# Reversed score rows of the odd tiles: put in order by a store to memory and a row gather, in place of two products with a reversal matrix

## The chip, the cores and the metric

The kernel runs on one core of a Trainium2 chip. The metric is the device time of one execution in microseconds (us), lower being better. Two chained blocks of a transformer-like model are computed for 512 tokens of width 1024, all in float32; large products are made as three products of rounded halves (high by high, low by high, high by low).

## The reference, cut to what matters

The second block contains a gated linear attention. Only its scores matter here; the kernel works in chunks of 128 tokens, which gives the same result as the reference's 64.

```python
def gla_chunked(q, k, v, log_f):
    ...
    def step(state, inp):
        qb, kb, vb, gb = inp
        cum = jnp.cumsum(gb, axis=-2)
        diff = cum[..., :, None, :] - cum[..., None, :, :]
        decay = jnp.exp(jnp.where(causal, diff, -jnp.inf))
        scores = jnp.einsum('bhtd,bhsd,bhtsd->bhts', qb, kb, decay)
        o_intra = jnp.einsum('bhts,bhsv->bhtv', scores, vb)
        o_inter = jnp.einsum('bhtd,bhdv->bhtv', qb * jnp.exp(cum), state)
        ...
        return new_state, o_intra + o_inter
```

## The kernel before

The 512 tokens are four tiles of 128. The first 51 weight blocks (n = 0 to 50) are taken in an order written out by hand. For each block every engine has its own straight list: SyncE loads the raw weights, ScalarE rounds them to the high half (`split`, helper line L1252), VectorE subtracts to get the low half (`lower`, L1808), TensorE multiplies (`fm_block`, through `three`, lines L594 to L596) and ScalarE and VectorE drain the banks. Beside each block an engine's `side(n)` does a piece of the attention work. In TensorE's list `side(n)` comes before the block's products, except for the blocks in `MID`, where it comes between the block's two tiles.

The gated attention's scores SC (16 tiles of 128x128, index head * 4 + token tile, rows are source tokens) are made level by level: n = 26 to 37 multiply (`gla_pairs`, L942) and VectorE merges the product under a mask (`level_merge`, L2188). For the odd token tiles the keys were reversed (KREV, KEP), so that the rows of the odd score tiles stand in reverse order. The level merges end in block 37. Then:

- n = 38 (GO - 2), TensorE: `scores_turn`, two products of the 128x128 reversal matrix by four odd score tiles each (L951) into banks 6 and 7.
- n = 39 (GO - 1), TensorE: `kdec_turn` (16 transposes of the decayed keys, L749). ScalarE: two copies of banks 6 and 7 back to SC (L1467), `chunk_split(0)` and `chunk_split(1)` (high halves of the values, L1385, and of the scores, L1386), then four copies of the transposed keys (L1475). VectorE: the low halves of the same (L1808), in `chunk_split` and `k_dec_lower`.
- n = 40 (GO) and after, TensorE: `gla_out(j)` for j = 0 to 3, which for j = 0 waits until the four transposed banks are drained by `k_dec_lower`. ScalarE squares the output (L1394), GpSimd computes the reciprocal root (`rstd`, L2850 and L2851), VectorE scales by it. ScalarE and VectorE split chunk j + 2 beside `gla_out(j)`.

GpSimd's list is short: the small roots, the loads with accumulation, a few broadcasts. Between the last root of the layer norm in block 33 and the first of `gla_norm` in block 40 it has nothing. `x1_spilled` is the semaphore of an earlier store of the residual to memory (16 when done, L2905). `tables_in` counts three small table loads at the start, the last of them the reversal matrix (L3000).

Of the kernel before, what the change touches and what calls it, by code (L numbers as in the profile page):

```python
# [15 lines left out]
P = 128  # L16
S = 512
# [84 lines left out]
def two_blocks(nc, a, out, x1_spill, m_spill):  # L102
# [47 lines left out]
    REVERSAL = place("reversal", [P, P])  # L150
# [64 lines left out]
    KEP = at("k_decayed_left_halves", [P, H * S // 2], XS + 16 * K1)  # L215
    KREV = at("k2_odd_tiles_reversed", [P, H * S // 2], XS + 12 * K1)
# [93 lines left out]
    with ctx:  # L310
# [258 lines left out]
        def two(t):  # L569
            return t.rearrange("p (t c) -> p t c", t=2)  # L570

# [6 lines left out]
        def _(pe):  # L578
# [366 lines left out]
            def scores_turn():  # L945

                for half in range(2):
                    drained(pe, ("lv", LEVELS - 1, half))
                for i in range(2):
                    dst = take(6 + i, ("scR", i))  # L950
                    give(pe.matmul(quarters(dst[:, :]), REVERSAL[:, :], SC[:, 2 * i + 1::TT, :], start=True, stop=True), ("scR", i))  # L951

# [111 lines left out]
            def side(n):  # L1064
# [14 lines left out]
                if n == GO - 2: scores_turn()  # L1079
# [153 lines left out]
        def _(act):  # L1233
# [149 lines left out]
            def chunk_split(j):  # L1383

                act.activation(V2H[:, j, :], V2[:, j, :], ACT.Copy).then_inc(chunk_hi, 1)  # L1385
                act.activation(SCH[:, :, j, :], SC[:, j::TT, :], ACT.Copy).then_inc(chunk_hi, 1)  # L1386
# [20 lines left out]
            def side(n):  # L1407
# [55 lines left out]
                if n == GO - 1:  # L1463
                    act.wait_ge(kd_done, 1)
                    for i in range(2):
                        b = full(act, ("scR", i))
                        ins = act.activation(SC[:, 2 * i + 1::TT, :], quarters(b[:, :]), ACT.Copy)  # L1467
                        free(ins, ("scR", i))
                    for i in range(2):
                        drained(act, ("scR", i))  # L1470
                    chunk_split(0)
                    chunk_split(1)
# [324 lines left out]
        def _(dve):  # L1797
# [409 lines left out]
            def chunk_split(j):  # L2207
# [4 lines left out]
                lower(SCL[:, :, j, :], SC[:, j::TT, :], SCH[:, :, j, :]).then_inc(chunk_lo, 1)  # L2212
# [624 lines left out]
        def _(pool):  # L2837
# [85 lines left out]
            for j in range(TT):  # L2923
                pool.wait_ge(ln_var, j + 1)
                rstd(RST[:, j:j + 1], MV[:, j, 1:2], 1, 1.0, LN_EPS)
            for j in range(TT):
# [29 lines left out]
        def _(sp):  # L2956
# [43 lines left out]
            sp.dma_start(REVERSAL[:, :], a["c_reversal"]).then_inc(tables_in, 16)  # L3000
# [81 lines left out]
def constants():  # L3082
# [3 lines left out]
    for l in range(LEVELS):  # L3086
# [6 lines left out]
            "c_masks": masks, "c_reversal": (s == P - 1 - t).astype(np.float32), "c_pool_edge": edge.astype(np.float32)}  # L3093
# [33 lines left out]
```

## Time and profile before

| what | value |
|---|---|
| median of 3 runs | 1060.89 us (1060.86 to 1061.44) |
| the profiled execution, its own time | 1060.83 us |
| its span, first to last instruction | 1059.0 us |
| TensorE matmul busy | 1049.3 us, 99% of the span |
| VectorE, ScalarE, GpSimd busy | 73%, 51%, 9% |
| mean granted TensorE clock | 0.999 of 2.4 GHz |

The span and the execution's own time differ by 1.83 us, which lies outside the instructions. A busy share says how full an engine's row is; the waits of an engine say whether it was ever late; and the chain that ended last says which engine's work, in order of time, adds up to the span.

### The profile page before, as it was taken

What the parts mean: (1) busy time and instruction counts of PE and PEld (TensorE: products, weight loads), DVE (VectorE), ACT (ScalarE), POOL (GpSimd) and SP (SyncE); (2) the same over time, 40 slices, a digit from 0 to 9 for tenths busy, and PEclk for the clock granted to TensorE, in tenths of its full rate; (3) what the DMA queues carried; (4) which work ended last, traced back from release to release, by engine and by line L of the source; (5) the groups of instructions that cost most, each with busy time, mean ns of one, the idle gap of its engine ahead of it and who ended that gap; (6) DMA issues with size and microseconds to landing.
All of it is one profiled execution on the core that took longest, in us unless ns stands there. A gap on an engine that the chain in (4) does not pass through costs nothing.

```text
span 1059.0 us, 13875 instructions
## 1 busy us (share of the span) xinstructions
PE 1049.3 (99%) x5688; PEld 906.5 (86%) x5688; DVE 777.9 (73%) x878; ACT 536.0 (51%) x620; POOL 91.5 (9%) x106
## 2 busy tenths in 40 slices
PE   9999999999999999999999999999999999999997
PEld 8788888888888888888888888888999999888885
DVE  5778856547976787777877455588887777897897
ACT  7575642453544644255434633352656656655560
POOL 1301000000012010001100000014000000220200
PEclk9999999999999999999999999999999999999999
DMA  9847412223863755323222222262132343999962
GB/s 325 242 114 166 145 52 74 90 80 105 212 141 108 219 121 160 119 80 100 82 78 80 80 80 80 102 218 79 50 111 80 103 137 121 179 206 251 180 218 80
DMA packets 95775, 138.89 MB, mean 131 GB/s; under 512 B 4988, under 2 KB 59772, under 8 KB 95584
## 3 DMA queue, kind: packets, MB, share of 16 engines
q1 hardware_dynamic: 77808, 97.49, 28.1%
q0 software_dynamic: 17616, 40.38, 18.8%
q8 instruction: 45, 0.74, 0.3%
q10 hardware_dynamic: 288, 0.13, 0.1%
q14 instruction: 18, 0.15, 0.0%
HBM read 133.79 MB, written 4.20 MB: 130 GB/s over the span
## 4 chain that ended last, share of the span: by engine, by line
PE 92%; DVE 4%; ACT 2%; DMA 1%; issue 1%; SPq 0%; DVEq 0%
PE bank L594 28%; PE bank L596 28%; PE bank L595 28%; PE bank L749 2%; DVE w_ff_lo L1808 1%; ACT w_ff_hi L1493 1%; PE bank L942 1%; PE bank L868 1%; PE bank L848 1%; PE bank L999 1%; PE bank L901 1%; PE bank L886 1%; DMA w_raw<-in_w_mem_kv 1%; PE bank L974 0%; DVE w_raw L2449 0%
## 5 line engine op out<-in xcount | busy, mean ns | idle before, releaser
L1808 DVE TENSOR_TENSOR w_lo<-w_raw,w_hi 128x2048 fp32r<-128x2048 f32 (+2 forms) x81 | 174.7, 2158 | 118.3 <-ACT w_hi L1252 97.8
L594 PE MATMUL bank<-act_t_hi,w_hi 128*128 128x512 f32 (+1 forms) x592 | 226.9, 383 | 0.0
L596 PE MATMUL bank<-act_t_hi,w_lo 128*128 128x512 f32 (+1 forms) x592 | 223.8, 378 | 0.0
L595 PE MATMUL bank<-act_t_lo,w_hi 128*128 128x512 f32 (+1 forms) x592 | 223.6, 378 | 0.0
L596 PEld LDWEIGHTS bank<-act_t_hi,w_lo 128*128 128x128 f32 x592 | 111.3, 188 | 20.9
L595 PEld LDWEIGHTS bank<-act_t_lo,w_hi 128*128 128x128 f32 x592 | 111.4, 188 | 20.4 <-issue 0.5
L594 PEld LDWEIGHTS bank<-act_t_hi,w_hi 128*128 128x128 f32 x592 | 111.4, 188 | 20.5 <-issue 0.5
L1252 ACT ACTIVATE w_hi<-w_raw 128x2048 fp32r<-128x2048 f32 (+1 forms) x48 | 88.9, 1854 | 31.8 <-PE bank L596 31.8
L594 PE MATMUL bank<-w_hi,hidden_hi 128*128 128x512 f32 x216 | 84.1, 389 | 0.0
L596 PE MATMUL bank<-w_hi,hidden_lo 128*128 128x512 f32 x216 | 84.0, 389 | 0.0
L595 PE MATMUL bank<-w_lo,hidden_hi 128*128 128x512 f32 x216 | 84.0, 389 | 0.0
L1808 DVE TENSOR_TENSOR w_ff_lo<-w_raw,w_ff_hi 128x1024 fp32r<-128x1024 f32 x49 | 59.9, 1223 | 28.3 <-ACT w_ff_hi L1493 28.3
L1493 ACT ACTIVATE w_ff_hi<-w_raw 128x1024 fp32r<-128x1024 f32 x49 | 51.7, 1056 | 43.6 <-DVE w_raw L2453 18.4
L1709 ACT ACTIVATE w_hi<-w_raw 128x2048 fp32r<-128x2048 f32 x28 | 53.5, 1911 | 30.3 <-DMA w_raw<-in_w_ff 26.5
L594 PE MATMUL bank<-act_t_hi,w_ff_hi 128*128 128x256 f32 x224 | 63.6, 284 | 0.4 <-DVE ff_hidden L2704 0.4
L596 PE MATMUL bank<-act_t_hi,w_ff_lo 128*128 128x256 f32 x224 | 63.4, 283 | 0.0
L595 PE MATMUL bank<-act_t_lo,w_ff_hi 128*128 128x256 f32 x224 | 63.4, 283 | 0.0
L596 PEld LDWEIGHTS bank<-w_hi,hidden_lo 128*128 128x128 f32 x216 | 40.5, 188 | 8.5
L595 PEld LDWEIGHTS bank<-w_lo,hidden_hi 128*128 128x128 f32 x216 | 40.5, 188 | 8.4
L594 PEld LDWEIGHTS bank<-w_hi,hidden_hi 128*128 128x128 f32 x216 | 40.5, 188 | 8.4 <-DVE w_lo L1808 0.2
L594 PE MATMUL bank<-h_sum_hi,w_ff_hi 128*128 128x256 f32 x168 | 47.5, 283 | 0.0
L595 PE MATMUL bank<-h_sum_lo,w_ff_hi 128*128 128x256 f32 x168 | 47.5, 283 | 0.0
(407 smaller groups left out, 2275.6 us busy)
## 6 DMA issues: line engine op xcount, KB each, us to landing
w_raw<-in_w_in SPq DMA_DIRECT2D x38, 1024.0 KB, 5.3
w_raw<-in_w_ff POOLq DMA_DIRECT2D x16, 1024.0 KB, 14.9
w_raw<-in_w_ff SPq DMA_DIRECT2D x28, 512.0 KB, 4.2
w_raw<-in_w_ff SPq DMA_DIRECT2D x13, 1024.0 KB, 8.3
w_vo_sums<-in_w_in POOLq DMA_DIRECT2D x8, 1024.0 KB, 9.2
w_raw<-in_w_out SPq DMA_DIRECT2D x8, 1024.0 KB, 5.1
w_vo_sums<-in_w_in SPq DMA_DIRECT2D x6, 1024.0 KB, 5.4
w_out_sums<-in_w_out POOLq DMA_DIRECT2D x4, 1024.0 KB, 8.9
```

Source lines behind the costliest of these rows:

```text
L594: pe.matmul(dst, lh, rh, start=start, stop=False, skip_group_check=onto)
L595: pe.matmul(dst, lh, rl, start=False, stop=False, skip_group_check=onto)
L596: return pe.matmul(dst, ll, rh, start=False, stop=stop, skip_group_check=onto)
L749: last = pe.transpose(dst[:, tile_of(i)], src(i), IDENT[:, :])
L848: last = pe.matmul(bank[b][:, c0:c0 + S - i * P], QK[:, 4 + h, tile_of(i)], QK[:, h, i * P:S], start=True, stop=True)
L868: last = pe.matmul(dst[:, c:c + P + 1], PP[h % 2][:, w:w + P], V[:, i, h, :], start=i == 0, stop=i == j)
L886: last = pe.matmul(dst[:, q:q + NMEM], QC[:, h, tile_of(j)], KM[:, h, :], start=True, stop=True)
L901: last = pe.matmul(dst[:, tile_of(h)], VM[:, m, tile_of(h)], PT[j % 2][:, 2 * h + m, :], start=m == 0, stop=m == MT - 1)
L1252: act.activation(WH[slot_of(n)][:, c0:w], raw_of(n)[:, c0:w], ACT.Copy).then_inc(w_hi, 1)
L1493: act.activation(UPH[g % FF1_SLOTS][:, :, :], up_place(i), ACT.Copy).then_inc(up_hi, 1)
L1709: act.activation(MH[split_slot(p)][:, :], MRAW[s][:, :], ACT.Copy).then_inc(w_hi, 1)
L1808: return dve.tensor_tensor(dst, src, hi.bitcast(f32), ALU.subtract)
```

## The change

The two products, ScalarE's two copies of them, and ScalarE's wait for its own copies are gone. GpSimd's queue, after the last root of the layer norm, waits until the last merge is done, stores the odd score tiles to memory (128 rows of 8 pieces of 512 B, 512 KB), waits until that store has landed and until the product ("sg", 7) is done (it read the table WST, whose place is used for the gather's target), and gathers the 128 rows of 4 KB back in reversed order into a new tile SCO. ScalarE waits for the gather ahead of `chunk_split(1)`, and the splits of chunks 1 and 3 read SCO. The table load of 64 KB becomes one of 128 row numbers.

```diff
-    REVERSAL = place("reversal", [P, P])
+    ROWS = place("reversed_rows", [P, 1], mybir.dt.uint32)
...
+    SCO = at("gla_scores_odd_tiles", [P, H, TT // 2, P], A + 72 * K1)
...
+        def scores_of(j):
+            return SCO[:, :, j // 2, :] if j % 2 else SC[:, j::TT, :]
...
-            def scores_turn():
-
-                for half in range(2):
-                    drained(pe, ("lv", LEVELS - 1, half))
-                for i in range(2):
-                    dst = take(6 + i, ("scR", i))
-                    give(pe.matmul(quarters(dst[:, :]), REVERSAL[:, :], SC[:, 2 * i + 1::TT, :], start=True, stop=True), ("scR", i))
...
-                if n == GO - 2: scores_turn()
...
-                act.activation(SCH[:, :, j, :], SC[:, j::TT, :], ACT.Copy).then_inc(chunk_hi, 1)
+                act.activation(SCH[:, :, j, :], scores_of(j), ACT.Copy).then_inc(chunk_hi, 1)
...
                     act.wait_ge(kd_done, 1)
-                    for i in range(2):
-                        b = full(act, ("scR", i))
-                        ins = act.activation(SC[:, 2 * i + 1::TT, :], quarters(b[:, :]), ACT.Copy)
-                        free(ins, ("scR", i))
-                    for i in range(2):
-                        drained(act, ("scR", i))
                     chunk_split(0)
+                    act.wait_ge(x1_spilled, 16 * 3)
                     chunk_split(1)
...
-                lower(SCL[:, :, j, :], SC[:, j::TT, :], SCH[:, :, j, :]).then_inc(chunk_lo, 1)
+                lower(SCL[:, :, j, :], scores_of(j), SCH[:, :, j, :]).then_inc(chunk_lo, 1)
...
+            for half in range(2):
+                drained(pool, ("lv", LEVELS - 1, half))
+            pool.dma_start(s_spill.rearrange("p (c t) -> p c t", t=P), SC[:, 1::2, :]).then_inc(x1_spilled, 16)
+            pool.wait_ge(tables_in, 16 * 3)
+            pool.wait_ge(x1_spilled, 16 * 2)
+            full(pool, ("sg", 7))
+            pool.indirect_dma_start(SCO[:, :, :, :].rearrange("p h c t -> p (h c t)"), None, s_spill[:, :],
+                                    bass.IndirectOffsetOnAxis(ROWS[:, :], 0)).then_inc(x1_spilled, 16)
...
-            sp.dma_start(REVERSAL[:, :], a["c_reversal"]).then_inc(tables_in, 16)
+            sp.dma_start(ROWS[:, :], a["c_rows"]).then_inc(tables_in, 16)
```

## Rows read from the trace of the kernel before

**Rows 1.** Busy time of each engine, share of the span, instructions.
```profile
PE 1049.3 (99%) x5688; PEld 906.5 (86%) x5688; DVE 777.9 (73%) x878; ACT 536.0 (51%) x620; POOL 91.5 (9%) x106
```
**Rows 2.** Waits of all engines: waiter, releaser, us in total, times, longest.
```profile
PE bank L594 <- DVE w_lo L1808: 1.0, 1, 1.0
PE bank L594 <- DVE ff_hidden L2704: 0.4, 2, 0.3
...
ACT w_hi L1709 <- DMA w_raw<-in_w_ff: 26.5, 12, 4.1
```
**Rows 3.** Chain that ended last, 564 to 580 us: start, us, what.
```profile
564.94 1.79 PE bank L999 x16
...
577.62 1.72 PE bank L951 x4
579.34 0.23 PE bank L594
```
**Rows 4.** The instructions of line L951: duration ns min/median/max, first and last start.
```profile
L951 PE MATMUL bank<-gla_scores,reversal x4: 591/592/592, 577.5 to 578.7; 128*128 128x512 f32 x4
```
**Rows 5.** TensorE in order of time, 577 to 580 and 602.75 us: start, us.
```profile
577.24 0.39 PE L596 MATMUL bank<-act_t_hi,w_lo 128*128 128x512 f32 x1
...
578.78 0.79 PE L594 MATMUL bank<-act_t_hi,w_hi 128*128 128x512 f32 x1
579.41 0.39 PE L595 MATMUL bank<-act_t_lo,w_hi 128*128 128x512 f32 x1
...
602.75 0.28 PE L594 MATMUL bank<-v_hi,gla_scores_hi 128*128 128x256 f32 x1
```
**Rows 6.** ScalarE in order of time, block 39: start, us.
```profile
592.69 1.07 ACT L1467 ACTIVATE gla_scores<-bank 128x512 f32<-128x512 f32 x2
593.86 1.06 ACT L1385 ACTIVATE v_hi<-v 128x1024 fp32r<-128x1024 f32 x1
...
595.34 1.04 ACT L1385 ACTIVATE v_hi<-v 128x1024 fp32r<-128x1024 f32 x1
```
**Rows 7.** GpSimd in order of time, 600 to 623 us; in brackets the idle time before.
```profile
606.99 0.84 POOL L2850 TENSOR_SCALAR rstd_tmp<-mean_squares 128x4 f32<-128x4 f32 x1 [84.49 <-ACT gla_o L1394]
...
621.68 0.20 POOL L2850 TENSOR_SCALAR rstd_tmp<-mean_squares 128x4 f32<-128x4 f32 x1 [12.76 <-ACT gla_o L1394]
```
**Rows 8.** VectorE in order of time, 568 to 608 us.
```profile
568.82 1.31 DVE L2188 COPY_PREDICATED gla_scores<-level_masks,bank 128x512 f32<-128x512 uint8 x1
...
575.01 2.29 DVE L2199 TENSOR_TENSOR decay<-cum 128x2048 f32<-128x2048 f32 x1
...
583.42 2.29 DVE L2205 TENSOR_TENSOR k_decayed<-k,decay 128x2048 f32<-128x2048 f32 x1 [0.94 <-ACT decay L1462]
...
596.78 1.22 DVE L1808 TENSOR_TENSOR v_lo<-v,v_hi 128x1024 fp32r<-128x1024 f32 x1
...
598.52 2.47 DVE L1808 TENSOR_TENSOR k_dec_t_lo<-bank,k_dec_t_hi 128x512 fp32r<-128x512 f32 x4
605.48 2.29 DVE L1808 TENSOR_TENSOR w_lo<-w_raw,w_hi 128x2048 fp32r<-128x2048 f32 x1 [4.49 <-ACT w_hi L1252]
```
**Rows 9.** GpSimd's issue of a transfer of 512 pieces of 512 B.
```profile
194.39 0.83 POOL L2887 DMA_DIRECT2D pool_w_sb<-in_pool_w  x1 [1.02 <-DVE mlstm_h L2054]
```
**Rows 10.** DMA issues of GpSimd's queue: count, KB each, median us to landing.
```profile
x_spill<-residual POOLq DMA_DIRECT2D x1, 2048.0 KB, 12.7
...
ln_b_all<-in_ln_b POOLq DMA_DIRECT2D x2, 512.0 KB, 14.2
...
w_s_by_source<-in_w_s_by_source POOLq DMA_DIRECT2D x1, 512.0 KB, 3.7
...
m_spill<-m_rows POOLq DMA_DIRECT2D x1, 8.0 KB, 4.1
```
**Rows 11.** Stretches: us, busy PE, PEld, DVE, ACT, POOL, clock, DMA share, GB/s.
```profile
568.00:573.00 5.00, 5.00 (x24) 4.15 (x23) 4.93 (x7) 3.88 (x4) 0.00 (x0) 1.00 0.61 179
573.00:578.00 5.00, 5.00 (x23) 3.98 (x22) 4.87 (x3) 0.34 (x1) 0.00 (x0) 1.00 0.09 31
```

More of the change, by code:

```diff
@@ L99, in block_list, with two_blocks @@
     return blocks
-def two_blocks(nc, a, out, x1_spill, m_spill):
+def two_blocks(nc, a, out, x1_spill, m_spill, s_spill):
+    import concourse.bass as bass
     from concourse import mybir
@@ L3092, in constants @@
     return {"c_ident": (s == t).astype(np.float32), "c_triu": (s <= t).astype(np.float32),
-            "c_masks": masks, "c_reversal": (s == P - 1 - t).astype(np.float32), "c_pool_edge": edge.astype(np.float32)}
+            "c_masks": masks, "c_rows": (P - 1 - s).astype(np.uint32), "c_pool_edge": edge.astype(np.float32)}
 def vector_columns(i):
@@ L3123 @@
     m_spill = nc.dram_tensor("m_spill", (H, S), mybir.dt.float32, kind="Internal").ap()
-    two_blocks(nc, a, out, x1_spill, m_spill)
+    s_spill = nc.dram_tensor("s_spill", (P, H * S // 2), mybir.dt.float32, kind="Internal").ap()
+    two_blocks(nc, a, out, x1_spill, m_spill, s_spill)
     r = run_bass_kernel_spmd(nc, [arrays], core_ids=[0])
```

## The prediction

> **What bounds the kernel now.** I read the busy times first: TensorE's matmul row is full, 1049.3 of 1059.0 us, and no other engine is above 73% [rows 1]. A full row need not be the bound, so I read the waits next. TensorE's waits are few: two groups with work of other engines, 1.0 us in the first blocks and 0.4 us in the feed-forward part [rows 2], none of them near the change. Third, the chain that ended last: around 577 us it consists of TensorE alone, and it holds the two products with the reversal matrix as one piece of 1.72 us, directly between ordinary products [rows 3]. So what TensorE no longer has to do in this stretch comes off the end, as long as nothing that it needs later becomes late.
>
> **What is removed from TensorE.** The two products are four records, two passes each [rows 4]. I price them by starts, not by durations, since the durations overlap. The ordinary product before them starts at 577.24, the next ordinary one is recorded at 578.78 but the one after that only at 579.41 [rows 5]. Ordinary starts are one chain piece of 0.23 us apart [rows 3], so without the products the step from 577.24 to 579.41 would take two pitches, 0.46 us, instead of 2.17: 1.71 us saved. The chain shows 1.72 [rows 3]. Bounds: not less than four ordinary pitches, 0.9 us, for four passes of the same 512 columns; not more than the four recorded durations, 4 x 0.592 = 2.37 us [rows 4]. I take 1.72, since two readings give it.
>
> **What is removed from ScalarE.** Two copies out of the banks take 1.07 us together, and with the hand-over 593.86 - 592.69 = 1.17 us pass before the values' split begins [rows 6]. ScalarE isn't on the path that sets the end here, so this is no gain in itself. I cost it at nothing, for TensorE's work hides it; it only gives ScalarE 1.17 us of room. Were that cover gone, it would be worth 1.17 us more.
>
> **What is added, and the room it has.** GpSimd has been idle for 84.49 us when its root at 606.99 begins, so nothing is queued behind its new waits until then [rows 7]. Its first wait ends with the last merge, 568.82 + 1.31 = 570.13 [rows 8]. The other wait, for the product ("sg", 7), ends with the group at 564.94 + 1.79 = 566.73 [rows 3], earlier, and costs nothing.
> Issue of the store: 1,024 pieces of 512 B. The nearest issue row, 512 such pieces, is 0.83 us [rows 9]; twice that is 1.7, my value.
> Store to landing: from below 4.1 us (the 8 KB store), from above 12.7 us (the 2 MB one) [rows 10]. It starts inside a weight load, since the DMA engines are 61% busy in 568 to 573 us and 9% in the next 5 [rows 11]. I take 6 us, near the small one: a quarter of the 2 MB transfer's bytes would be 3.2 us. Landed at 570.1 + 1.7 + 6 = 577.8.
> Gather, issue and landing: no row shows a gather. The nearest are loads of 512 KB into 128 rows, 3.7 us with free engines and 14.2 us at worst [rows 10]; a gather computes 128 addresses from a table, so I add 1 to 2 us and take 5.5 us. Landed at 583.3. With both transfers at their lower ends it is 570.1 + 1.7 + 4.1 + 3.7 = 579.6; with both at their upper ends, and an issue of 1.7 and one of 0.8 us, 570.1 + 12.7 + 14.2 + 2.5 = 599.5.
> When it is wanted: ScalarE's order begins 1.72 us earlier than before (it follows TensorE's drains) and without the copies. The first values' split then begins at 592.69 - 1.72 = 590.97; it and the scores' split took 595.34 - 593.86 = 1.48 us to the next start, so the new wait is reached at 592.45 [rows 6]. The gather has 22.3 us from the merge to there, and by my sum needs 13.2.
>
> **What waits behind it if it is late.** Call its landing G. On ScalarE behind the wait stand the second values' split (1.04 us), the scores' split, and the four copies of the transposed keys. VectorE's order behind that takes 598.52 + 2.47 - 596.78 = 4.21 us from its split of the second values to its last low half of the keys [rows 8]. It would end at about G + 1.1 + 4.2 = G + 5.3. TensorE's `gla_out(0)` waits for this and is due at 602.75 - 1.72 = 601.03 [rows 5]. So TensorE stalls only if G is after 595.7; it has lost the whole 1.72 us if G is 597.4, and the kernel is slower than before by 0.2% (2.1 us) if G is 599.5. The squares, roots and scaling of the output would then be late with TensorE, by the same amount and not more.
>
> **A rule against the change.** GpSimd's small operation at 606.99 took 0.84 us, and the same one at 621.68 took 0.20 [rows 7]. By the Trainium skill (SBUF — State Buffer, "SBUF: two separate sides") GpSimd and VectorE share a pair of ports, and GpSimd cannot write the descriptors of its transfers while VectorE holds it. The two durations agree with such a lock, for the first ended at 607.83, right after VectorE's weight split from 605.48 to 607.77 [rows 8].
> Whatever holds GpSimd, the rows say what it would do: VectorE is busy 4.93 and 4.87 us of the two stretches of 5 us from 568 to 578 [rows 11], its last long operation there ending at 577.30 [rows 8]. If the store can't be issued until then, it lands at 577.3 + 1.7 + 4.1 to 12.7, thus 583.1 at best. The gather's issue may then meet the operation at 583.42, which ends at 585.71 [rows 8], and land at 585.7 + 0.8 + 3.7 = 590.2. That is still 2.3 us before it is wanted, 5.5 before TensorE stalls. With 6 us for the store and 5.5 for the gather it is 585.0 and 591.2. Only this hold together with transfers near their upper ends is late.
>
> **Small things.** The table load shrinks from 64 KB to 512 B at the start, where no wait of TensorE hangs on it: nothing. The added traffic, 1 MB, falls beside weight loads that are wanted a block or more later; nothing. The later stretches hang on TensorE's progress, since each load is released by a split and each split by a product, so they should move by the same 1.72 us.
>
> **The sum.** The profiled execution took 1060.83 us with a span of 1059.0. Span after: 1059.0 - 1.72 = 1057.3; its own time 1059.1. The median of the runs is 0.06 above the profiled execution, so 1059.2 us, 0.16% less. Differences under about 0.2% (2.1 us) of this kernel cannot be told from no change; the forecast lies just inside that.
>
> **The rivals.**
> - *Forecast: the gather is hidden, TensorE saves its 1.72 us.* For it: the rows of the chain and of the starts, 9 us of room. 1058.8 to 1059.7. Chance 0.64.
> - *The products cost TensorE more than their pitch.* The record behind them is 0.79 us long instead of 0.39 [rows 5], and their durations add up to 2.37 [rows 4]; if that last value comes off, 1060.89 - 2.37 = 1058.5, and with a few tenths more from ScalarE's freed time in the feed-forward part, 1058.3. Against it: the starts behind them are already back at the ordinary pitch. Chance 0.20, faster by over 0.2%.
> - *The gain is swallowed later.* In the feed-forward part ScalarE waits for weight transfers 12 times, 26.5 us in all, and TensorE lost 0.4 us to VectorE there [rows 2]. Were that part paced by something that doesn't move with TensorE, 1060.9 would stay. Against it: what is loaded there is released by products and splits. Chance 0.05.
> - *The gather comes too late, the other side.* Its place is ScalarE's wait ahead of chunk 1, its point G = 597.4. Both transfers at their upper ends, free issue: G = 599.5, stall 3.8 us, time 1059.2 + 3.8 = 1063.0. With the issue held until 577.3 besides, G = 577.3 + 1.7 + 12.7 + 0.8 + 14.2 = 606.7, stall 11.0, time 1070.2. For it: no row shows a gather's price, and GpSimd can be held. Against it: the upper ends come from a transfer of four times the bytes and from moments with busy DMA engines, and here they are nearly free from 573 on [rows 11]. Chance 0.11, of which 0.02 lies between the thresholds and 0.09 beyond.
>
> **How the numbers follow.** Time 1059.2. Faster by over 0.2%: the second case, 0.20. Slower by over 0.2%: the last case's larger part, 0.09. Within: 0.64 + 0.05 + 0.02 = 0.71. The range for 8 times in 10 has the likeliest case and most of the second one; 1058.4 leaves out a little of the latter below, and 1060.4 leaves out the swallowed and the late cases above, 0.16 in all.
>
> **What the profile after would show.** The chain of TensorE around 577 us without the 1.72 us piece, and `gla_out(0)` at 601.0 instead of 602.75. GpSimd's store at 570.2, the gather's issue at 577 to 578 (past 583 if VectorE holds it), its landing by 584. ScalarE without a wait for DMA ahead of its second values' split, at about 592.5. TensorE's waits as before. The forecast is wrong if ScalarE shows a wait for DMA there of more than 3.2 us, or if a new wait of TensorE appears in the feed-forward part.

## The result, and the profile after

The changed kernel takes 1062.65 us (median of 22 runs, 1061.40 to 1066.67), the kernel before 1060.91 us in runs beside them (median of 22, 1060.39 to 1061.70). The ratio is 1.002, with a 95% interval of 1.0014 to 1.0026: slower by 1.74 us, where 1.7 us less was forecast. 1062.65 lies outside the range of 1058.4 to 1060.4. The profiled execution took 1062.58 us with a span of 1060.8 us.

Start as for the kernel before, with the busy times of the page [rows 1]:

```profile
PE 1048.0 (99%) x5684; PEld 905.8 (85%) x5684; DVE 777.7 (73%) x878; ACT 535.1 (50%) x618; POOL 94.2 (9%) x108
```

TensorE is busy 1.3 us less and yet the span is 1.8 us longer, so TensorE must wait more. The waits of TensorE say where (waiter, releaser, us in total, times, longest):

```profile
PE bank L599 <- DVE ff_hidden L2695: 3.4, 2, 1.9
PE bank L762 <- POOL v_and_ones L2853: 1.0, 1, 1.0
PE bank L599 <- DVE w_lo L1799: 0.7, 1, 0.7
PE bank L599 <- DVE u_gelu L2476: 0.4, 1, 0.4
```

The first group was 0.4 us [rows 2] and is 3.4 now: two waits, at 795 and 857 us, in the first feed-forward stage, 200 us behind the change. The last group is new, and it is in the stretch of the change.

**Where the 1.77 us arise.** Four marks of the chain that ended last, in both kernels. After:

```profile
594.54 1.53 PE bank L754 x14
...
795.59 0.36 PE bank L599
...
857.77 0.36 PE bank L599
...
1053.35 0.24 PE bank L601
```

In the kernel before the same pieces start at 595.71, 795.01, 855.96 and 1051.58. So the new kernel is 1.17 us ahead when block 39 begins (0.12 of it stands already at 551 us, before the change), 0.58 behind at 795, 1.81 behind at 857 and 1.77 behind at the end. It gained 1.17 us and then lost 1.75 and 1.23 us at two places, together 2.98, which is the growth of the first wait group, 3.4 - 0.4 = 3.0.

**The gather is hidden.** GpSimd in order of time, and the landing of its two transfers (KB each, us to landing):

```profile
570.59 0.91 POOL L2919 DMA_DIRECT2D s_spill<-gla_scores  x1 [48.21 <-DVE gla_scores L2179]
576.09 2.04 POOL L2923 DMA_INDIRECT gla_scores_odd_tiles<-s_spill,reversed_rows  x1 [4.59 <-issue]
```
```profile
s_spill<-gla_scores POOLq DMA_DIRECT2D x1, 512.0 KB, 4.7
gla_scores_odd_tiles<-s_spill,reversed_rows POOLq DMA_INDIRECT x1, 5.3
```

The gather lands at 576.09 + 5.3 = 581.4. ScalarE, in order of time, reaches the wait more than 11 us later and goes on without a pause (no bracket with idle time):

```profile
592.46 0.62 ACT L1382 ACTIVATE gla_scores_hi<-gla_scores 128x512 fp32r<-128x512 f32 x1
592.98 1.05 ACT L1381 ACTIVATE v_hi<-v 128x1024 fp32r<-128x1024 f32 x1
593.93 0.62 ACT L1382 ACTIVATE gla_scores_hi<-gla_scores_odd_tiles 128x512 fp32r<-128x512 f32 x1
```

**Part of the gain is lost at once.** TensorE, and then VectorE, in order of time:

```profile
577.11 0.39 PE L601 MATMUL bank<-act_t_hi,w_lo 128*128 128x512 f32 x1
577.93 0.47 PE L599 MATMUL bank<-act_t_hi,w_hi 128*128 128x512 f32 x1 [0.42 <-DVE u_gelu L2476]
578.23 0.39 PE L600 MATMUL bank<-act_t_lo,w_hi 128*128 128x512 f32 x1
```
```profile
572.58 2.28 DVE L2184 TENSOR_TENSOR q_decayed<-q,decay 128x2048 f32<-128x2048 f32 x1
574.89 2.29 DVE L2190 TENSOR_TENSOR decay<-cum 128x2048 f32<-128x2048 f32 x1
577.10 0.68 DVE L2476 TENSOR_TENSOR u_gelu<-u_gelu,bank 128x512 f32<-128x512 f32 x1
```

VectorE takes 4.5 us of attention work before it drains a bank of block 37, and TensorE needs that bank for block 38. The product due at 577.11 + 0.23 = 577.34 starts at 577.93, and the step behind it is 0.30 us instead of 0.23: 0.66 us lost. In the kernel before the two products with the reversal matrix stood exactly there and covered the drain. From the piece of 16 transposes at 551 us to the one of block 39 the kernel before takes 595.71 - 551.37 = 44.34 us, this one 594.54 - 551.25 = 43.29. That is 1.05 us saved, and with the 0.66 it is the 1.71 priced.

**The larger part is lost in the first feed-forward stage.** Here SyncE's queue loads half blocks (512 KB each), and six times it issues three such loads within 2.4 us; they are called groups 1 to 6 below, and pairs 1 to 6 in the texts recorded ahead of the experiments. The chain that ended last, before 795 us:

```profile
782.48 1.15 DVE w_raw L2450
783.62 0.02 issue
783.64 6.21 DMA w_raw<-in_w_ff
...
789.94 1.24 DVE w_raw L2440
...
794.76 0.69 DVE ff_hidden L2695
...
795.59 0.36 PE bank L599
```

The transfer in the chain is the first load of group 2. In the kernel before, the chain of this stretch holds no transfer at all. The first load of group 2 by its source line (issue duration ns, first and last start us), after and then before:

```profile
L3036 SPq DMA_DIRECT2D w_raw<-in_w_ff x1: 367/367/367, 783.6 to 783.6; - x1
...
DMA to landing us min/median/max: 6.2/6.2/6.2
```
```profile
L3037 SPq DMA_DIRECT2D w_raw<-in_w_ff x1: 367/367/367, 784.8 to 784.8; - x1
...
DMA to landing us min/median/max: 4.2/4.2/4.2
```

The same 512 KB take 6.2 us instead of 4.2. The load is even issued 1.1 us earlier (the forecast had 1.7), and lands 0.9 us later. At group 5 it is again so: the chain holds `846.15 5.87 DMA w_raw<-in_w_ff`, before `845.57 4.64`. VectorE is what waits for these loads, 1.6 us each time; before, 0.4 in all (waits of 740 to 860 us, after and then before):

```profile
DVE w_raw L2440 <- DMA w_raw<-in_w_ff: 3.3, 2, 1.6
```
```profile
DVE w_raw L2449 <- DMA w_raw<-in_w_ff: 0.4, 1, 0.4
```

VectorE makes the half block and the activation `ff_hidden` late, and TensorE waits for that, 1.9 and 1.5 us.

**What is in the way of the load.** The changed kernel moves no other data near 784 us. The queues of the DMA engines in 784.7 to 786.9 us, right behind the issue (packets, MB, share of 16 engines):

```profile
q1 hardware_dynamic: 610, 0.61, 90.0%
q8 instruction: 1, 0.02, 6.5%
```

One packet of queue 8 is among the load's packets. It starts at 785.51 us and occupies its DMA engine for 2.30 us, where the median of the 45 is 1.06. In the kernel before, the corresponding packet starts at 785.30 us, 0.5 us ahead of the loads' first packets: by their starts, the stretch 784.8 to 785.8 holds that packet alone, and 785.8 to 788 holds only the loads (the packet itself lasts until 786.37):

```profile
q8 instruction: 1, 0.02, 6.7%
```
```profile
q1 hardware_dynamic: 599, 0.60, 92.0%
```

The traces also show how the load is late. From 789.8 to 791.8 us, when the last load of group 2 is being finished, and in the matching stretch of the kernel before (791.0 to 793.0 us):

```profile
q1 hardware_dynamic: 48, 0.05, 6.8%
```
```profile
q1 hardware_dynamic: 7, 0.01, 0.9%
```

Nearly everything of the three loads has arrived at 789.8, and what is left comes one 1 KB packet after the other: 6.8% is about the share of one engine of 16. The third load lands behind this, at 785.99 + 6.55 = 792.5 us. So it looks as if one DMA engine were some 2 us behind the other fifteen. The profile doesn't name the engine of a packet, so that it is the one that had carried queue 8's packet is not shown.

Queue 8 moves 45 packets in both kernels (page, the queues):

```profile
q8 instruction: 45, 0.74, 0.3%
```

That is 16 KB each. TensorE's list has about 11,640 instructions, 259 for each packet, and no other engine's list is nearly as long. The packets come every 14 to 33 us, closest together in the first feed-forward stage, where TensorE's products are the shortest. Counted in TensorE's instructions instead of time they are even: in the kernel before, from the 28th packet to the last, 4357 recorded instructions start in 17 steps, 256 for each, single steps between 219 and 297. I take them for the fetches of TensorE's instructions. The change takes 10 instructions out of that list (four weight loads, four matmuls and two semaphore instructions; the page's total falls by ten as well, from 13875 to 13865, since ScalarE has four fewer and GpSimd four more), so each later fetch comes at another point of TensorE's work. This is the theory that the experiments below test; I call it the fetch theory.

By the Trainium skill (Runtime: NRT & Kernel Launch, "Instruction fetch mechanics") an engine's instruction memory is refilled in blocks of 16 KiB, 256 instructions, by a DMA queue of the engine's own, and the cost of this is mostly hidden. The size agrees, and so do the 256 instructions from packet to packet. The traces show no wait of TensorE for the fetch itself either; what is not hidden is the delay of a data transfer that the fetch meets.

### The profile page after: what moved, and what is told of

It is laid out like the page before. It is cut to its first block, busy times and chain, and to the rows that moved or that the text cites. A ratio compares the mean times of both kernels' runs of the same rounds, so it can differ in the third digit from the quotient of the medians.

```text
span 1060.8 us, 13865 instructions
## 1 busy us (share of the span) xinstructions
PE 1048.0 (99%) x5684; PEld 905.8 (85%) x5684; DVE 777.7 (73%) x878; ACT 535.1 (50%) x618; POOL 94.2 (9%) x108
## 4 chain that ended last, share of the span: by engine, by line
PE 91%; DVE 4%; DMA 2%; ACT 2%; issue 1%; SPq 0%; DVEq 0%
PE bank L599 27%; PE bank L601 27%; PE bank L600 27%; PE bank L754 2%; DVE w_ff_lo L1799 1%; ACT w_ff_hi L1484 1%; DMA w_raw<-in_w_ff 1%; PE bank L947 1%; PE bank L873 1%; PE bank L853 1%; PE bank L906 1%; PE bank L891 1%; DMA w_raw<-in_w_mem_kv 1%; PE bank L996 1%; PE bank L971 0%
```

## Experiments

Times are medians of the runs in one session with their range; "beside" is the kernel before on the same chip. Ratios are to it, with a 95% interval. Instructions were added to TensorE's list as waits on a semaphore that has long been reached; every two of them make one instruction in the trace. The rivals of the fetch theory are: the traffic or the queue of the store and gather disturbs the loads; the time at which TensorE comes to the stretch, earlier or later, does it; or TensorE's drain wait moves everything.

**1. The change with ten instructions put back** (at TensorE's start, ahead of all its work).

```diff
                     pe.matmul(bank[7][:, 0:P], ONES[:, :], ONES[:, :], start=True, stop=True)
+                for _ in range(20):
+                    pe.wait_ge(ones_set, 1)
```

> The changed kernel with ten instructions more at the head of TensorE's list (waits that are met at once, behind the warm-up), so that from there to the feed-forward part TensorE's list has as many instructions ahead of any product as the kernel before. Theory F (the 16 KB transfers of TensorE's instructions fall at another place against the weight loads of the feed-forward part, because TensorE's list got ten instructions shorter): the two late landings go, 1.1 us saved of the kernel before, about 1059.8 us. Theory M (the store, the gather or the place of tensors in memory makes the later loads slow): stays at 1062.6 us. Theory P (shorter work ahead of the feed-forward part by itself puts it in a bad phase): stays at 1062.6 us.

1060.04 us (1059.39 to 1060.44, 11 runs) beside 1060.77; ratio 0.9991 [0.9982, 1.0]. Waits of TensorE:

```profile
PE bank L599 <- DVE u_gelu L2478: 0.4, 1, 0.4
PE bank L599 <- DVE ff_hidden L2697: 0.3, 1, 0.3
```

The 3.4 us are down to 0.3, 2.6 us of time come back, and not one instruction of work differs. The fetch again starts alone, 0.5 us ahead of the loads (queues in 783.8 to 784.8 us):

```profile
q8 instruction: 1, 0.02, 8.8%
```

The drain wait of 0.4 us stays, and the stretch of block 39 is entered at 594.69, as in the change. So the two losses are separate. The first load of group 2 is issued at 783.77 us, where the change has 783.64, and lands after 4.6 us instead of 6.2: TensorE comes to the place at the same time, so that time isn't the cause.

**2. The kernel before with ten instructions fewer** (three warm-up matmuls fewer, which are 12 instructions, and two instructions of waits).

```diff
-WARM_UP = 18
+WARM_UP = 15
...
+                for _ in range(4):
+                    pe.wait_ge(ones_set, 1)
```

> The kernel before with ten instructions fewer at the head of TensorE's list (three of the 18 warm-up products, 12 instructions, less two added ones). No part of the change is in it. Theory F: the feed-forward part gets the late landings of the changed kernel, 1062 to 1064 us. Theories M and P: 1060.9 us, since neither traffic nor work near the change differs.

1063.63 us (1063.43 to 1066.05, 5 runs); ratio 1.0035 [1.0022, 1.0049].

```profile
PE bank L594 <- DVE ff_hidden L2706: 2.6, 2, 1.4
```

The wait appears in a kernel that has neither store nor gather and still has the two products. In this execution 0.65 us of the loss are something else: the first piece of 16 transposes starts at 30.14 instead of 29.49 us, behind a longer wait for the first weights.

**3. The change without the store and the gather.** GpSimd's block and ScalarE's wait are taken out; the splits read SC, so the odd tiles' rows stay in reversed order.

```diff
-            pool.dma_start(s_spill.rearrange("p (c t) -> p c t", t=P), SC[:, 1::2, :]).then_inc(x1_spilled, 16)
...
-            pool.indirect_dma_start(SCO[:, :, :, :].rearrange("p h c t -> p (h c t)"), None, s_spill[:, :],
-                                    bass.IndirectOffsetOnAxis(ROWS[:, :], 0)).then_inc(x1_spilled, 16)
...
-                    act.wait_ge(x1_spilled, 16 * 3)
...
-            return SCO[:, :, j // 2, :] if j % 2 else SC[:, j::TT, :]
+            return SC[:, j::TT, :]
```

> The changed kernel without the store, the gather and ScalarE's wait; the splits of chunks 1 and 3 read the rows as they are, so the odd tiles' score rows stay in reversed order. What remains is TensorE's and ScalarE's part of the change. Theory F: like the changed kernel, 1062 to 1064 us. Theory M: 1059.8 us, 1.1 less than before. Theory P: like the changed kernel.

1062.93 us (1061.18 to 1064.47, 11 runs) beside 1060.77; ratio 1.0021 [1.0012, 1.003]. TensorE waits 3.7 us for `ff_hidden` in two waits. The loss does not need the traffic.

**4. The kernel before with the store and the gather added**, both products kept and the gather's result not read. ScalarE also waits for the store ahead of its two copies, and the small table of row numbers is loaded at the start (not shown).

```diff
+            pool.dma_start(s_spill.rearrange("p (c t) -> p c t", t=P), SC[:, 1::2, :]).then_inc(x1_spilled, 16)
...
+            pool.indirect_dma_start(SCO[:, :, :, :].rearrange("p h c t -> p (h c t)"), None, s_spill[:, :],
+                                    bass.IndirectOffsetOnAxis(ROWS[:, :], 0)).then_inc(x1_spilled, 16)
...
+                    act.wait_ge(x1_spilled, 16 * 3)
                     chunk_split(1)
```

> The kernel before with the store and the gather added on GpSimd's queue; the gathered tile is not read, the two products stay, and ScalarE waits for the store ahead of its copies and for the gather ahead of chunk 1. TensorE's list is as before. Theory F: 1060.9 us. Theory M: 1063 to 1065 us, above the changed kernel by the 1.1 us of TensorE's products. Theory P: 1060.9 us.

1060.82 us (1060.37 to 1061.38, 11 runs) beside 1060.77; ratio 1.0 [0.9991, 1.0009]. The traffic costs nothing, and with experiment 3 it is out as a cause of this loss.

**5. Ten instructions put back, and the bank drained first.** VectorE's `k_dec_arg` (the operation of 2.29 us) moves from ahead of the drains of block 37 to between them.

```diff
                     q_cum()
-                    k_dec_arg()
...
                     for key, c in fm:
+                        if n == GO - 3 and c % 2: k_dec_arg()
                         dve.wait_ge(ga_sig, c + 1)
```

> As the changed kernel with ten instructions more at the head, and VectorE's argument of the keys' decay (2.3 us) moved from ahead of the two drains of block 37 to between them, so that the bank which TensorE takes for block 38 is free about 2.3 us earlier. Theory D (the two products hid this drain, and without them TensorE waits for it, 0.42 us idle and some tenths of restart): the wait at 577.9 us goes and about 0.6 us with it, 1059.4 us. Rival (the idle time is replaced by another wait, or the drain isn't what it waits for): 1060.0 us.

1058.79 us (1058.35 to 1059.36, 11 runs) beside 1060.65; ratio 0.9981 [0.9972, 0.999]. VectorE in order of time:

```profile
574.90 0.68 DVE L2478 TENSOR_TENSOR u_gelu<-u_gelu,bank 128x512 f32<-128x512 f32 x1
575.50 2.29 DVE L2192 TENSOR_TENSOR decay<-cum 128x2048 f32<-128x2048 f32 x1
```

The drain is 2.2 us earlier, TensorE's wait for it is gone, and block 39 begins 593.96 - 551.37 = 42.59 us after the mark: 1.75 us less than the 44.34 of the kernel before. This is the gain as forecast, undisturbed, and the fastest of all the kernels; it beats both. Against experiment 1 the stretch is 0.67 us shorter (43.26 there); the medians differ by 1.25 us, and the rest of that is not accounted for.

**6. Ten instructions put back, but behind the place** (in TensorE's second feed-forward stage, ahead of its second product).

```diff
             for p in range(PRODUCTS - 2):
+                if p == 1:
+                    for _ in range(20):
+                        pe.wait_ge(ones_set, 1)
                 product_ready(p)
```

> The changed kernel with the same ten instructions placed behind the feed-forward part's first stage, after the first product of its second stage. Theory F (what counts is how many of TensorE's instructions stand ahead of the first stage's products): nothing mended, 1062 to 1064 us plus at most 0.5 us for the instructions themselves. Rival I (the length or the place of the whole instruction list in memory counts): mended as in the run with ten at the head, about 1060.0 us.

1062.59 us (1061.44 to 1065.08, 11 runs) beside 1060.65; ratio 1.0023 [1.0014, 1.0032]; `ff_hidden` 3.2 us in two waits. The same list length as in experiment 1, without its effect, with the first load of group 2 issued at 783.73 us, again at the same time: what counts is how many instructions stand ahead of the loads, and not the length of the list.

**7. Forty instructions put in.** As in experiment 1, with 40 of the 80 waits placed behind `km_part(0, 2, 4)`, to lengthen the list without making the start longer. Experiments 8, 9, 12 and 13 do the same with 60 waits there.

```diff
+                for _ in range(40):
+                    pe.wait_ge(ones_set, 1)
...
                     km_part(0, 2, 4)
+                    for _ in range(40): pe.wait_ge(ones_set, 1)
```

> The changed kernel with 40 instructions more at the head, 30 beyond the number that the kernel before has. Theory F: at 0.06 us for each instruction of the stage the transfers come 1.8 us earlier against the loads than in the kernel before, at about 783.5 and 845.1 us, ahead of the loads of pairs 2 and 5 and with the tail of those of pairs 1 and 4: no late landing that TensorE waits for, 1059.7 to 1060.5 us. Theory N (only the exact old number is good; any other is slow): 1062 us or more.

1059.64 us (1059.24 to 1060.6, 11 runs) beside 1060.65; ratio 0.9991 [0.9982, 1.0]. `ff_hidden` 0.2 us. The fetches of groups 2 and 5 are 1.3 and 1.5 us ahead of the loads' first packets, and the gain doesn't grow with them.

**8. Eighty instructions**, meant to push the fetches of groups 1 and 4 into their loads.

```diff
+                for _ in range(100):
+                    pe.wait_ge(ones_set, 1)
...
+                    for _ in range(60): pe.wait_ge(ones_set, 1)
```

> The changed kernel with 80 instructions more at the head, 70 beyond the kernel before. Theory F: the transfers come 4.2 us earlier against the loads than in the kernel before, so that they fall into the first half of the loads of pairs 1 and 4 (765 to 770 and 827 to 831 us) and clear of those of pairs 2 and 5: TensorE's waits move to those pairs, 1.5 to 3 us in all, and the time is 1061.5 to 1063.5 us, with 1 us more if the added instructions at the start aren't hidden. Theory G (more instructions ahead is simply better): 1060 us or less plus that start.

1063.06 us (1062.48 to 1064.73, 10 runs); ratio 1.0022 [1.0013, 1.0032]. The time is as slow as the change's, and for another reason: `ff_hidden` is 0.2 us, and TensorE waits 3.2 us at its start, where the first piece of 16 transposes is at 33.18 instead of 29.85 us (experiment 5). Without that it would be about 1059.7. The fetches fell 3.3 and 2.7 us behind the first packets of groups 1 and 4, and their first loads landed after 3.7 us, so the forecast of moved waits was missed. But the second loads landed after 6.2 and 6.3 us instead of 4.7 to 4.8, and nothing waited for those.

**9. A hundred and twenty-five instructions.**

```diff
+                for _ in range(190):
+                    pe.wait_ge(ones_set, 1)
...
+                    for _ in range(60): pe.wait_ge(ones_set, 1)
```

> The changed kernel with 125 instructions more at the head. In the run with 80 the two transfers began 3.3 and 2.7 us after the first packets of the three loads of pairs 1 and 4, and TensorE had no wait there. 45 instructions more should bring them to about 1 us after, inside the first of the three loads. Theory F1 (what counts is that the transfer falls into the first of the three loads, in whichever pair): waits of TensorE for ff_hidden of 1 us or more beside pairs 1 or 4 (near 775 to 785 or 835 to 845 us on this kernel's clock, which starts about 6 us late), none beside 2 and 5. Theory F2 (pairs 2 and 5 alone have no slack): no such wait. The time is 1065.5 us without waits, from 1059.6 us and 5.9 us of added start, and 2 to 3 us more with them.

1068.41 us (1068.34 to 1068.53, 4 runs); ratio 1.0073. The fetches of groups 1 and 4 were 1.1 and 1.0 us ahead of the loads, not in them, and `ff_hidden` is 0.2 us. The loss is at the start, where the padding has become too long: TensorE waits 7.8 us, the granted clock is 0.5 (1.2 GHz) for the 6.83 us from 12.6 to 19.5 us, and the first piece of 16 transposes is at 38.87 instead of 29.85 us.

**10. The change with the bank drained first**, the list length untouched.

```diff
-                    k_dec_arg()
...
+                        if n == GO - 3 and c % 2: k_dec_arg()
```

> The changed kernel with only VectorE's order mended (the keys' decay argument between the two drains of block 37), no instructions added. Theory: both causes add up; the drain gives back 0.7 us and more (1.2 us between the two runs with ten at the head), the late landings stay: 1061.4 to 1062 us. Rival (mending either is enough): 1059 us.

1061.99 us (1061.37 to 1064.09, 11 runs) beside 1060.75; ratio 1.0015 [1.0006, 1.0024]. `ff_hidden` 3.2 us in two waits. The drain's wait is gone and some time with it (0.66 us between the medians), the larger loss stays: the fetches start 0.8 and 1.1 us into the loads. So it isn't the drain that made the loads late.

**11. The kernel before with the bank drained first.** The edit of experiment 10 on the kernel before.

```diff
-                    k_dec_arg()
...
+                        if n == GO - 3 and c % 2: k_dec_arg()
```

> The kernel before with VectorE's order mended in the same way. Theory D (the two products cover this drain): nothing gained, 1060.8 us. Rival (the mended order is a gain of its own): 1060.0 us or less.

1060.80 us (1060.4 to 1061.38, 11 runs) beside 1060.75; ratio 1.0001 [0.9992, 1.001]. An early drain is worth nothing while the two products cover a late one.

**12. A hundred instructions.**

```diff
+                for _ in range(140):
+                    pe.wait_ge(ones_set, 1)
...
+                    for _ in range(60): pe.wait_ge(ones_set, 1)
```

> The changed kernel with 100 instructions more at the head. With 80 the transfers began 3.3 and 2.7 us after the first packets of the loads of pairs 1 and 4, with 125 they began 1.1 and 0.9 us ahead of them, and in neither did TensorE wait there; by interpolation 100 puts them 1.3 and 1.1 us after, inside the first of the three loads. Theory F1 (any pair whose first load is hit is late): waits of TensorE for ff_hidden of 1 us or more beside pairs 1 and 4, landings of 5.5 us or more of their first loads. Theory F2 (pairs 2 and 5 alone lack the slack): first loads late, but no such wait. About 1065.5 us without waits (5.9 us of added start), 1067.5 to 1069 us with them.

1065.73 us (1065.45 to 1066.25, 4 runs); ratio 1.0049. Missed again: the fetches were 0.4 and 0.5 us ahead of the loads of groups 1 and 4, and `ff_hidden` is 0.2 us. TensorE's wait at the start is 5.0 us. Experiment 13 takes ten instructions less, so that the fetches come later.

**13. Ninety instructions.**

```diff
+                for _ in range(120):
+                    pe.wait_ge(ones_set, 1)
...
+                    for _ in range(60): pe.wait_ge(ones_set, 1)
```

> The changed kernel with 90 instructions more at the head. With 80 the transfers began 3.3 and 2.7 us after the first packets of the three loads of pairs 1 and 4, with 100 they began 0.4 and 0.5 us ahead; 90 should put them 1 to 1.5 us after. Theory F1 (any pair): first loads of these pairs land after 5.5 us or more, and TensorE waits for ff_hidden beside them, 1 us or more each. Theory F2 (pairs 2 and 5 alone lack the slack): late first loads without such waits. 1064 to 1065 us without waits (4.5 to 5 us of added start), 2 to 3 us more with them.

Two runs, 1065.64 and 1068.54 us; 4.1 us of it are the wait at the start. Now the fetches lie 1.9 and 2.6 us behind the first packets of groups 1 and 4. Waits of TensorE, and the chain that ended last around group 4:

```profile
PE bank L599 <- DVE ff_hidden L2698: 1.6, 2, 1.5
```
```profile
828.78 6.12 DMA w_raw<-in_w_ff
...
839.82 0.69 DVE ff_hidden L2698
...
840.64 0.36 PE bank L599
```

The first load of group 4 lands after 6.1 us instead of 3.7, and a wait of 1.5 us stands where no other kernel of this study has one; the waits at groups 2 and 5 are down to 0.2 us in all. So, in this one profiled execution, the loss was moved to another place by the list length alone. At group 1 the first load landed after 3.7 us all the same, the second after 6.2, and no wait came.

**14. Forty instructions and the bank drained first.** Experiments 7 and 10 together.

```diff
+                for _ in range(40):
+                    pe.wait_ge(ones_set, 1)
...
+                    for _ in range(40): pe.wait_ge(ones_set, 1)
...
+                        if n == GO - 3 and c % 2: k_dec_arg()
```

> The changed kernel with 40 instructions more at the head and VectorE's order mended. If both causes are what the earlier runs say, this equals the run with 40 less the 0.7 us and more of the drain: 1058.4 to 1058.9 us, faster than the kernel before by 0.2%. If the gain of the version with ten hung on one place alone, 1059.5 us or more.

1058.90 us (1058.57 to 1059.55, 11 runs) beside 1060.43; ratio 0.9985 [0.9976, 0.9994]. As good as experiment 5, at another list length that keeps the fetches ahead of the loads.

**The positions together.** Start of the fetch minus the first data packet of the group of loads, from the packets in the trace, in order of the time that TensorE waits for `ff_hidden`:

```
kernel                        group 2  group 5  wait for ff_hidden, us
3  change, no traffic          +2.2     +0.1     3.7 in 2
change (after)                 +0.8     +2.0     3.4 in 2
10 change, drain first         +0.8     +1.1     3.2 in 2
6  change, +10 behind          +1.0     +1.9     3.2 in 2
2  before, -10                 +1.3     +1.9     2.6 in 2
before                         -0.5     +0.2     0.4
11 before, drain first         -0.4     +0.0     0.3
1  change, +10                 -0.5     -0.6     0.3
4  before, + traffic           -0.4     +0.1     0.2
5  +10, drain first            -0.4     -0.6     0.2
14 +40, drain first            -1.0     -1.4     0.2
7  change, +40                 -1.3     -1.5     0.2
8  change, +80                 -3.5     -3.6     0.2
```

In experiments 9, 12 and 13 the fetches near groups 2 and 5 are 5 us and more ahead.

A fetch that starts ahead of the loads, or up to 0.2 us into them, costs TensorE 0.4 us at most; one that starts 0.8 to 2.2 us into them makes the first load late. In experiment 3 group 5 is an edge: +0.1, but the packet took 2.94 us and the load landed after 6.4 us.

The landings of all three loads say more (us from issue to landing, with the fetch's start as above and TensorE's wait for `ff_hidden` at that group):

```
kernel, group                    fetch   first  second  third   wait
before, 1: no fetch near           -      3.6    4.7     4.2     0
9  +125, group 1                 -1.1     3.8    6.3     5.7     0
14 +40 drain first, group 2      -1.0     3.7    6.1     5.5     0.2
1  +10, group 5                  -0.6     4.1    6.2     5.6     0
before, group 5                  +0.2     4.6    5.7     5.1     0.3
after, group 2                   +0.8     6.2    7.1     6.5     1.9
after, group 5                   +2.0     5.9    6.8     6.2     1.5
13 +90, group 1                  +1.9     3.7    6.2     5.6     0
13 +90, group 4                  +2.6     6.1    7.1     6.5     1.5
8  +80, group 4                  +2.7     3.7    6.3     5.6     0
```

So a fetch near a group nearly always makes some load late, by 0.5 to 2.5 us, also where it costs nothing. TensorE waits for more than 0.3 us only where the first of the three is late; where the first is on time and the second is late, it doesn't.

## Why the prediction was wrong, point by point

- **The products' price** was right. Priced at 1.72 us; measured 1.75 with the drain out of the way (experiment 5), 1.05 as changed.
- **"TensorE's waits as before"** was wrong in the stretch itself. The first step that failed, and the smaller one, is "what TensorE no longer has to do in this stretch comes off the end, as long as nothing that it needs later becomes late": I asked what would become later, and not what had been late all the time under the two products. VectorE's drain was; 0.66 us. [Rows 8] show the operation at 575.01 to 577.30 that holds it, and I used it only against GpSimd.
- **The rival that the products cost more** (2.37 us) is out: 1.75 measured at most.
- **The store and the gather** were hidden, as forecast, with more room than priced. Issue of the store 0.91 us (priced 1.7), landing 4.7 (priced 6), issue of the gather 2.04 and landing 5.3 with it (priced 5.5), landed at 581.4 (priced 583.3), wanted at 592.98 (priced 592.45). In all twelve kernels with the gather it took 5.2 to 6.2 us from issue to landing. That nothing in the rows gave its price didn't matter, with 11 us of room.
- **GpSimd held by VectorE** happened, at a smaller price than the rule case gave. The store was not held until 577.3: it was issued from 570.59 to 571.50. The gather's issue was begun inside VectorE's `decay` operation and ended 0.95 us after that one's end (576.09 + 2.04 = 578.13 against 574.89 + 2.29 = 577.18). In experiment 5 that operation starts 0.6 us later and ends at 577.79, and the issue takes longer, to 0.94 us behind it:

```profile
576.23 2.50 POOL L2925 DMA_INDIRECT gla_scores_odd_tiles<-s_spill,reversed_rows  x1 [4.60 <-issue]
```

The same in all twelve kernels with the gather: issues of 1.76 to 2.53 us, each ending 0.94 or 0.95 us behind that operation. By the Trainium skill (SBUF — State Buffer, "SBUF: two separate sides") GpSimd can't write its descriptors while VectorE holds the shared ports; the trace agrees for the gather. If an issue that nothing holds takes the 0.94 us, the hold was about 1 us (an estimate; no issue without VectorE's operation was seen), and with more than 11 us of room it cost nothing.
- **ScalarE's copies worth nothing**: right, no wait of TensorE on ScalarE is there after the change, as none was before.
- **"The later stretches hang on TensorE's progress … so they should move by the same 1.72 us"** is the step of the sum that failed, and it made the sign wrong. The loads did move with TensorE, by 1.1 us at 783.6. What the runs showed in its place: the first loads of groups 2 and 5 land after 6.2 and 5.9 us, TensorE waits 3.4 us instead of 0.4, and ten idle instructions ahead take this away (experiment 1). By the fetch theory TensorE's own instruction fetches didn't move with the loads, since they hang on the count of instructions ahead, and two of them fell into a group of loads.
- **"Differences under about 0.2% cannot be told from no change"** was too wide: with 22 runs of each the interval of the ratio is 0.0006 to either side, and the 1.74 us lie outside it.
- **"The gain is swallowed later"**, chance 0.05, was the nearest rival, and both its cause (a stretch paced by something else) and its size (no more than the gain) were too small. A loss beyond the gain without a late gather was in none of the cases, so the chance of slower, 0.09, stood on the gather alone.
- What would show the forecast wrong was named, "a new wait of TensorE appears in the feed-forward part", and this is what the profile after shows.

The sum as it should have been: 1060.91 - 1.71 + 0.66 + 2.98 = 1062.84, against 1062.65 measured. Experiment 1 takes off the 2.98 (1059.86; measured 1060.04), experiment 5 both losses (1059.20; measured 1058.79, where the kernel beside it was at 1060.65).

**What stays open.** Experiments 1, 2 and 6 show that the number of instructions ahead of the loads turns the loss on and off, and one execution of experiment 13 that it moves it. In a late group the traces show the share of about one DMA engine still moving when the rest is done. That it is the engine of the fetch, and that the fetch's packet puts it behind, is argued from position, not shown. The packet's own duration doesn't account for it: it is 2.30 us in the case shown, but in 7 of the 11 cases with a late first load it is 0.88 to 1.55 us, hardly more than elsewhere, and the load is late by about 2 us all the same. What decides whether the first or the second load of a group is late is open too: at +1.9 in group 1 of experiment 13 and +2.7 in group 4 of experiment 8 it was the second, at +2.0 and +2.6 elsewhere the first. And four forecasts of a fetch's position (experiments 8, 9, 12 and in part 13) missed; the single steps of 219 to 297 instructions between fetches, where 256 is the mean, are enough for misses of 1 to 2 us there, where 256 instructions take about 15.5 us. Moving the loads instead of the fetches was not tried.

## What to carry to other kernels

Taking work off a full engine uncovers what it had covered: before pricing it at its own length, look which drain or load was late beneath it. In this kernel a change of ten instructions in the longest list shifted the later packets that I take for instruction fetches, and where loads stand close to their need this moved the time by more than the change itself; so read a small difference only after the same kernel was run with some idle instructions added ahead. When a kernel comes out slower far from its edit, compare the landing times of single loads before looking for a cause in the data.

## What the runs showed of the hardware that was not expected

- Beside a 16 KB packet of queue 8, taken for an instruction fetch, a 512 KB load landed after 6.2 us instead of 4.2. From 789.8 to 791.8 us the DMA engines were 6.8% busy with the rest of the loads, which is about one of 16. The packet itself took 2.30 us there, 0.88 to 1.55 us in most of the other cases.
- Ten instructions without work in TensorE's list change the time from 1062.65 to 1060.04 us. With a hundred (experiment 12) TensorE's wait for its first weights at the start is 5.0 us, where the kernel before has 1.0, so they were not free there.
- A gather of 128 rows of 4 KB took 5.3 us from its issue to landing. Its issue takes 1.76 to 2.53 us in the twelve kernels that have it, and ends 0.94 to 0.95 us after VectorE's running operation does in each; a store of 1,024 pieces of 512 B took 0.91 us to issue, where 512 such pieces had taken 0.83 [rows 9]. The issue time did not go with the number of pieces.
- The changed kernel spreads more, 1061.4 to 1066.7 us over 22 runs, against 1060.4 to 1061.7 of the kernel before, and the granted clock divides its runs: the five slowest, 1063.96 us and more, have a mean of 0.996 or 0.997, the other seventeen, up to 1063.51 us, 0.998 or 0.999. The profiled executions of experiments 3 and 10 (1064.20 and 1064.05 us, medians 1062.93 and 1061.99) show what can lie behind this. TensorE had waited 2.0 and 1.8 us for `ff_hidden`, then worked for 0.6 and 0.1 us, and then the clock stood at 0.5 (1.2 GHz) for 3.41 us. Experiment 10, stretches: us, busy PE, PEld, DVE, ACT, POOL, clock, DMA share, GB/s:

```profile
792.40:795.80 3.40, 1.59 (x14) 1.41 (x13) 3.05 (x3) 0.81 (x1) 0.00 (x0) 1.00 0.00 0
795.80:799.20 3.40, 3.40 (x17) 3.40 (x18) 3.12 (x4) 2.76 (x5) 0.00 (x0) 0.50 0.00 0
799.20:802.60 3.40, 3.40 (x30) 3.40 (x30) 1.66 (x2) 2.06 (x3) 0.00 (x0) 1.00 0.00 0
```

  17 matmuls are in the middle stretch and 30 in the one behind it, 0.12 us apart there, so the low clock costs some 1.5 us on top of the wait. Not every such wait is followed by it: the profiled execution of the changed kernel waited 1.9 and 1.5 us and kept its clock.
